# State space chunks with outputs turned in the product and the decay spread from bfloat16 parts; the first two output tiles fed piece by piece

## The reference, cut to what matters

```python
def ssd_chunked(x, dt, a, bm, cm, d_skip):
    xd = (x * dt[..., None]).reshape(bsz, nc, l, g, e, p)
    da = (dt * a).reshape(bsz, nc, l, g, e).transpose(0, 3, 4, 1, 2)
    cs = jnp.cumsum(da, axis=-1)
    seg = cs[..., :, None] - cs[..., None, :]
    decay = jnp.exp(jnp.where(tril, seg, -jnp.inf))
    cb = jnp.einsum("bclgn,bcsgn->bcgls", cm, bm)
    y_diag = jnp.einsum("bcgls,bgecls,bcsgep->bclgep", cb, decay, xd)
    decay_states = jnp.exp(cs[..., -1:] - cs)
    states = jnp.einsum("bclgn,bgecl,bclgep->bcgepn", bm, decay_states, xd)
    chunk_decay = jnp.exp(cs[..., -1])
    ...  # prev: states carried over the chunks, state * chunk_decay + new
    y_off = jnp.einsum("bclgn,bcgepn,bgecl->bclgep", cm, prev, jnp.exp(cs))
    return (y_diag + y_off).reshape(bsz, s, h, p) + x * d_skip[:, None]
# even_layer
    y = y * silu(z_a); y_a = rmsnorm of each group of 256 columns of y
    u = causal_dwconv(glu_v * sigmoid(glu_g), dw_w, dw_b)       # 31 taps
    y_b = silu(layernorm(u)) * silu(z_b)
    return x + jnp.concatenate([y_a, y_b], axis=-1) @ w_out
```

## Time and profile before

| | |
|---|---|
| median of 3 executions | 3494.46 us (3489.35 to 3498.19) |
| the profiled execution, its own time | 3493.44 us |
| its span, from first to last instruction | 3491.7 us |
| granted TensorE clock, mean over the span | 0.953 |
| TensorE busy / weight loads | 3156.6 us (90%) / 2493.5 us (71%) |
| VectorE, ScalarE, GpSimd busy | 1757.9, 978.6, 836.1 us |
| `block_even` | from about 1718 to 2690 us of the span |

### The profile page before, as it was taken

How to read it: one execution, slowest core, us unless ns; L and a number is a source line. 1 busy time by engine, 2 the same in 40 slices (tenths; PEclk the granted TensorE clock), 3 DMA queues, 4 the chain that set the end, 5 groups by cost and what they waited for, 6 DMA issues and landing times. The chain is left out here.

```text
span 3491.7 us, 38580 instructions
## 1 busy us (share of the span) xinstructions
PE 3156.6 (90%) x15262; PEld 2493.5 (71%) x15262; DVE 1757.9 (50%) x2675; ACT 978.6 (28%) x1839; POOL 836.1 (24%) x500
## 2 busy tenths in 40 slices
PE   5999988888899999999899999997798999999869
PEld 3777777666687787787678787875576777777647
DVE  4234566534532132233476868786343357777751
ACT  2332344314321010011233233332131244444430
POOL 1221000341332233332233333332122221111002
PEclk8998999999899999999899999999899999999889
DMA  2112000110111111112211111111222100000011
GB/s 103 37 36 88 13 1 13 37 49 29 44 48 44 47 48 42 49 47 72 66 43 49 61 46 63 43 67 55 115 91 84 37 31 31 25 31 25 7 61 72
DMA packets 45274, 170.26 MB, mean 49 GB/s; under 512 B 5040, under 2 KB 5312, under 8 KB 43968
## 3 DMA queue, kind: packets, MB, share of 16 engines
q1 hardware_dynamic: 44832, 161.85, 13.6%
q0 software_dynamic: 288, 6.29, 0.4%
HBM read 145.06 MB, written 23.07 MB: 48 GB/s over the span
## 5 line engine op out<-in xcount | busy, mean ns | idle before, releaser
L176 PE MATMUL acc<-x_hi,w_hi 128*128 128x512 f32 x2064 | 859.6, 416 | 88.5 <-DVE x_lo L267 43.3
L169 POOL CAST w_hi<-w_raw 128x1024 fp32r<-128x1024 f32 x217 | 237.0, 1092 | 2519.3 <-PE acc L178 1464.4
L177 PE MATMUL acc<-x_lo,w_hi 128*128 128x512 f32 x2064 | 831.5, 403 | 0.0
L178 PE MATMUL acc<-x_hi,w_lo 128*128 128x512 f32 x2064 | 829.8, 402 | 0.0
L171 POOL TENSOR_TENSOR w_lo<-w_raw,w_hi 128x1024 fp32r<-128x1024 f32 x217 | 544.3, 2508 | 17.4
L176 PEld LDWEIGHTS acc<-x_hi,w_hi 128*128 128x128 f32 x2064 | 396.8, 192 | 211.1 <-issue 81.0
L178 PEld LDWEIGHTS acc<-x_hi,w_lo 128*128 128x128 f32 x2064 | 397.6, 193 | 97.8
L177 PEld LDWEIGHTS acc<-x_lo,w_hi 128*128 128x128 f32 x2064 | 398.9, 193 | 87.2 <-issue 1.2
L2225 DVE SCALAR_TENSOR_TENSOR acc<-ev_upad,cols,acc 128x1024 f32<-128x1024 f32 x232 | 298.1, 1285 | 4.2
L378 DVE TENSOR_TENSOR h<-h,acc 128x1024 f32 (+1 forms) x40 | 48.9, 1221 | 317.1 <-PE acc L178 317.1
L176 PE MATMUL aux<-x_hi,w_hi 128*128 128x512 f32 x448 | 191.9, 428 | 0.0
(11 more groups left out here) (491 smaller groups left out, 5068.5 us busy)
## 6 DMA issues: line engine op xcount, KB each, us to landing
w_raw<-in_stream SPq DMA_DIRECT2D x217, 512.0 KB, 3.4
h<-in_x SPq DMA_DIRECT2D x16, 512.0 KB, 8.7
spill_h<-h SPq DMA_DIRECT2D x8, 512.0 KB, 5.3
spill<-ev_zst SPq DMA_DIRECT2D x8, 512.0 KB, 3.1
h_even<-spill_h SPq DMA_DIRECT2D x8, 512.0 KB, 7.8
ev_zr<-spill SPq DMA_DIRECT2D x8, 512.0 KB, 3.5
spill_h<-h_even SPq DMA_DIRECT2D x8, 512.0 KB, 5.3
h<-spill_h SPq DMA_DIRECT2D x8, 512.0 KB, 6.5
```

What stands on the lines that cost most here:

```text
L169: pool.tensor_copy(k.w_hi[slot][:], k.w_raw[slot][:]).then_inc(k.w_split, 1)
L176: pe.matmul(out, w_hi, x_hi, start=start, stop=False)
L177: pe.matmul(out, w_hi, x_lo, start=False, stop=False)
L178: return pe.matmul(out, w_lo, x_hi, start=False, stop=stop)
```

## The change

- The cumulated log decays cs are split into three bfloat16 parts on VectorE (`spl`), turned once by eight bfloat16 matmuls and copied by ScalarE to csT, with a group's three parts of four heads in 12 rows of a block of 32 partitions. `decays` becomes four bfloat16 matmuls on 32 rows, one for each head, with a selection matrix `sel` as weights. GpSimd's `d_steps` and the mask matmul go; the mask is put on the scores by VectorE (cbm).
- `products` has x as weights (64 columns) and the mixed decays as moving data, so that the output comes out turned, on the partitions 0 to 63 for even heads and 64 to 127 for odd ones. The state part becomes one matmul for each head on the same output, with cp as moving data: C times the exponential of cs (ScalarE's new ecb, VectorE's new `spread`). L1897, tmp, ysb, ecs and `back` go; `add_y` stands right behind `combine`.
- The reload is issued as twelve transfers of one tile each, and TensorE takes the output tiles 0 and 1 together, block by block (`first_pair`), with the last group's total behind block 1.

The diff, cut; allocations and names of semaphores are left out:

```diff
@@ -1787,13 +1790,6 @@
...
-    def d_steps(g, c):
-        if g * TT + c:
-            pool.wait_ge(s["cbr"], g * TT + c)
-        else:
-            pool.wait_ge(s["tables"], 4)
-        pool.tensor_tensor(d4[:], k.upto.unsqueeze(1).broadcast_to([P, 4, P]), heads(da, g, c, P), ALU.mult).then_inc(s["d4_ready"], 1)
...
     def x_ends(g, c):
         if c == 0:
...
-        d_steps(g, 0)
...
-        d_steps(g, 1)
...
         for c in range(TT):
...
-            if c + 2 < TT:
-                d_steps(g, c + 2)
...
-    for i, x in enumerate((x_hi, x_lo)):
-        pool.dma_start(x[:, 0:6, :], k.spill_ya[i][:, 0:6, :]).then_inc(s["ya_back"], 16)
+    for q in range(6):
+        pool.dma_start(x_hi[:, q, :], k.spill_ya[0][:, q, :]).then_inc(back[q], 16)
+        pool.dma_start(x_lo[:, q, :], k.spill_ya[1][:, q, :]).then_inc(back[q], 16)
...
@@ -1850,6 +1843,8 @@
...
     def turn_x(g, i):
+        if i < 2:
+            pe.wait_ge(s["cs_copied"], 1)
...
@@ -1870,46 +1865,39 @@
...
     def decays(g, c):
...
-        pe.wait_ge(s["d4_ready"], g * TT + c + 1)
+        pe.wait_ge(s["ebc"], 7 * g + max(c - 1, 0))
         if c == 0:
...
-            pe.wait_ge(s["consts"], 2)
+            pe.wait_ge(s["consts"], 3)
...
-            pe.wait_ge(s["mixed"], g * TT + c)
-            if c >= 2:
-                pe.wait_ge(s["yadded"], g * TT + c - 1)
-        pe.matmul(S[0], k.ones, d4[:].rearrange("p h c -> p (h c)"), start=True, stop=False)
-        pe.matmul(four(S[0]), identr[:], maskr[:].unsqueeze(1).broadcast_to([P, 4, P]), start=False, stop=True)
-        pe.matmul(S[3][:, 256:384], cv[:, 2, cols], cv[:, 3, cols], start=True, stop=True).then_inc(s["cbr"], 1)
+            pe.wait_ge(s["cbm"], g * TT + c)
+        r = slice(32 * g, 32 * g + 32)
+        for h in range(4):
+            pe.matmul(S[0][:, h * P:(h + 1) * P], sel[r, h, :], csT[r, cols], start=True, stop=True)
+        pe.matmul(S[3][:, 0:P], cv[:, 2, cols], cv[:, 3, cols], start=True, stop=True).then_inc(s["cbr"], 1)
...
     def products(g, c):
...
+        pe.wait_ge(s["yadded"], g * TT + c)
...
         if c == 0:
...
-            pe.wait_ge(s["ysb_ready"], g * TT + c)
+            pe.wait_ge(s["cp_ready"], 7 * g + c)
...
-            pe.matmul(S[2][:, 0:256], cv[:, 3, c * P:(c + 1) * P], state[:].rearrange("p h c -> p (h c)"), start=True, stop=True)
-        for h in range(4):
-            mm = pe.matmul(S[1][:, h * 64:(h + 1) * 64], dec[:, c % 2, h, :], xtok[:, c, h * 64:(h + 1) * 64], start=True, stop=True)
+        outs = [S[1][64 * (h % 2):64 * (h % 2) + 64, h // 2 * P:(h // 2 + 1) * P] for h in range(4)]
+        for two in (range(0, 2), range(2, 4)):
+            for h in two:
+                mm = pe.matmul(outs[h], xtok[:, c, h * 64:(h + 1) * 64], dec[:, c % 2, h, :], start=True, stop=c == 0)
+            for h in two if c else ():
+                mm = pe.matmul(outs[h], state[:, h, :], cp[:, h, :], start=False, stop=True)
...
-    def back(g, c):
-        pe.wait_ge(s["ysb_ready"], g * TT + c + 1)
-        if c < TT - 1:
-            pe.wait_ge(s["mixed"], g * TT + c + 2)
-        else:
-            pe.wait_ge(s["yadded"], g * TT + c)
-        for j in range(2):
-            mm = pe.transpose(S[3][:, j * P:(j + 1) * P], ysb[:, 2 * j:2 * j + 2, :].rearrange("p h c -> p (h c)"), k.ident)
-        mm.then_inc(s["yT"], 1)
...
     def group_total(g):
...
@@ -1930,7 +1918,11 @@
...
-            pe.wait_ge(s["tables"], 4)
+            pe.wait_ge(s["tables"], 3)
+            pe.wait_ge(s["cs_split"], 6)
+            for t in range(TT):
+                mm = pe.matmul(S[t // 4][:, t % 4 * P:(t % 4 + 1) * P], spl[:, t].rearrange("p g r -> p (g r)"), k.ident_h, start=True, stop=True)
+            mm.then_inc(s["cs_turned"], 1)
...
@@ -1950,9 +1942,7 @@
...
             products(g, c)
-            feed(n // 3)
-            back(g, c)
-            feed(n - 2 * (n // 3))
+            feed(n - n // 3)
...
     def out_tile(i, xh, xl, ready):
@@ -1970,14 +1960,28 @@
...
-    def a_ready(q):
-        if q == 0:
-            pe.wait_ge(s["ya_back"], 32)
-            pe.wait_ge(s[EV[2 * EVEN_N - 1][0]], EV[2 * EVEN_N - 1][1])
-        if q == 6:
-            group_total(SSD_GROUPS - 1)
-            pe.wait_ge(s["y_hi"], SSD_GROUPS)
-            pe.wait_ge(s["y_lo"], SSD_GROUPS)
+    def first_pair():
...
+        pe.wait_ge(s[EV[2 * EVEN_N - 1][0]], EV[2 * EVEN_N - 1][1])
+        pe.wait_ge(s["yadded"], TT * SSD_GROUPS)
+        for q in range(KD):
+            if q < 6:
+                pe.wait_ge(back[q], 32)
+            else:
+                pe.wait_ge(s["y_hi"], SSD_GROUPS)
+                pe.wait_ge(s["y_lo"], SSD_GROUPS)
+            for i in range(2):
+                n = oa + i
+                if q == 0:
+                    pe.wait_ge(k.w_split, n * 2 + 2)
+                for c in range(2):
+                    cols = slice(c * HALF, (c + 1) * HALF)
+                    mm = product3(pe, slots[i][:, cols], k.w_hi[n % 2][:, q * P:(q + 1) * P], k.w_lo[n % 2][:, q * P:(q + 1) * P],
+                                  x_hi[:, q, cols], x_lo[:, q, cols], q == 0, q == KD - 1)
+                if q == KD - 1:
+                    mm.then_inc(k.lin_done, 1)
+            if q == 1:
+                group_total(SSD_GROUPS - 1)
...
     def nothing(q):
...
@@ -2072,6 +2079,9 @@
...
+        if c:
+            act.wait_ge(s["cp_ready"], 7 * g + c - 1)
+            act.activation(ecb[:].rearrange("p h c -> p (h c)"), S[0], ACT.Exp).then_inc(s["ebc"], 1)
...
     def square(g):
...
@@ -2115,11 +2124,12 @@
...
-            act.activation(ecs, cs, ACT.Exp).then_inc(s["tables"], 1)
...
+            act.wait_ge(s["cs_turned"], 1)
+            act.activation(csT[:], aux[:, 0:SEQ], ACT.Copy).then_inc(s["cs_copied"], 1)
...
@@ -2193,7 +2203,13 @@
...
-    dve.tensor_scalar(maskr[:], k.upto, -1.0, 2.0 ** 127, ALU.add, ALU.mult).then_inc(s["consts"], 1)
+    dve.memset(spl[:], 0.0).then_inc(s["cs_split"], 1)
+    dve.tensor_reduce(picks[:], k.ident.rearrange("p (g r) -> p g r", r=32)[:, :, 0:12].rearrange("p g (i h) -> p h g i", h=4),
+                      AX, ALU.add).then_inc(s["consts"], 1)
+    dve.wait_ge(s["consts"], 1)
+    dve.tensor_reduce(onehot[:], picks[:], AX, ALU.add).then_inc(s["consts"], 1)
+    dve.wait_ge(s["consts"], 2)
+    dve.tensor_copy(sel[:], onehot[:].unsqueeze(2).broadcast_to([P, 4, P])).then_inc(s["consts"], 1)
...
     def handler(i):
@@ -2251,33 +2267,35 @@
...
     def mix(g, c):
+        dve.wait_ge(s["cbr"], g * TT + c + 1)
+        if g * TT + c:
+            dve.wait_ge(s["mixed"], g * TT + c)
+        dve.tensor_tensor(cbm, S[3][:, 0:P], k.upto, ALU.mult).then_inc(s["cbm"], 1)
+        dve.wait_ge(s["cbm"], g * TT + c + 1)
...
-        dve.tensor_tensor(dec[:, c % 2], dec[:, c % 2], S[3][:, 256:384].unsqueeze(1).broadcast_to([P, 4, P]),
-                          ALU.mult).then_inc(s["mixed"], 1)
+        dve.tensor_tensor(dec[:, c % 2], dec[:, c % 2], cbm.unsqueeze(1).broadcast_to([P, 4, P]), ALU.mult).then_inc(s["mixed"], 1)
...
+    def spread(g, c):
+        dve.wait_ge(s["ebc"], 7 * g + c)
+        dve.tensor_tensor(cp[:], ecb[:], cv[:, 3, c * P:(c + 1) * P].unsqueeze(1).broadcast_to([P, 4, P]), ALU.mult).then_inc(s["cp_ready"], 1)
...
     def combine(g, c):
...
-        if c:
-            dve.tensor_tensor(tmp[:], four(S[2][:, 0:256]), heads(ecs, g, c, 64), ALU.mult).then_inc(s["chain"], 1)
-            if c < TT - 1:
-                dve.tensor_tensor(state[:], state[:], heads(cdec, g, c, 64), ALU.mult).then_inc(s["chain"], 1)
-            dve.wait_ge(s["chain"], 13 * g + 2 * c - 1)
-            dve.tensor_tensor(ysb[:], tmp[:], four(S[1][:, 0:256]), ALU.add).then_inc(s["ysb_ready"], 1)
-            if c < TT - 1:
-                dve.wait_ge(s["chain"], 13 * g + 2 * c)
-                dve.tensor_tensor(state[:], state[:], four(S[2][:, 256:512]), ALU.add).then_inc(s["state_ready"], 1)
-                dve.wait_ge(s["state_ready"], g * (TT - 1) + c + 1)
-        else:
+        if c == 0:
...
-            dve.tensor_copy(ysb[:], four(S[1][:, 0:256])).then_inc(s["ysb_ready"], 1)
+        elif c < TT - 1:
+            dve.tensor_tensor(state[:], state[:], heads(cdec, g, c, 64), ALU.mult).then_inc(s["chain"], 1)
+            dve.wait_ge(s["chain"], 6 * g + c)
+            dve.tensor_tensor(state[:], state[:], four(S[2][:, 256:512]), ALU.add).then_inc(s["state_ready"], 1)
+        if c < TT - 1:
+            spread(g, c + 1)
...
     def add_y(g, c):
-        dve.wait_ge(s["yT"], g * TT + c + 1)
         if c == 0:
...
-        dve.tensor_tensor(yy, yy, S[3][:, 0:256].rearrange("p (j c) -> p j c", j=2), ALU.add).then_inc(s["yadded"], 1)
+        dve.tensor_tensor(yy, yy, S[1][:, 0:256].rearrange("p (j c) -> p j c", j=2), ALU.add).then_inc(s["yadded"], 1)
...
     def multiply(g):
...
@@ -2339,11 +2357,20 @@
...
+            parts = [spl[:, :, :, 4 * i:4 * i + 4] for i in range(3)]
```

(12 more changed lines are left out.)

29 lines of the change are left out of this document (17 added, 12 removed).

## The result

The changed kernel takes 3434.3 us (median of 4 runs, 3430.5 to 3441.9) beside 3491.9 us of the kernel before (4 runs): a ratio of 0.983, with a 95% interval of 0.981 to 0.985, or 57.6 us less. The forecast was 3439 us. The profiled execution took 3430.5 us around a span of 3428.7, 63.0 us shorter than that of before. Where these 63 us lie is told by marks that both traces have: the first decays, the first decays of each later group, the first tap of the last tile of `zst`, the last input product, the first of the sums over eight tiles (L1998 before, L2005 after).

The account below looks back on a forecast made before the run. TensorE's queue was taken to set the pace; 20.9 + 7.8 + 11.5 - 2.5 + 18 = 55.7 us off the profiled 3493.4 gave 3437.7, plus 1.0 to the median: 3439 us, range 3424 to 3467.

Parts of the forecast that it names:

- the rival by which the gain comes back there: At the three group changes, TensorE's waits for ScalarE take back the gain of groups 0 to 2: 3460 us; chance 0.07.
- Decays: TensorE's decay visit in each chunk: 0.80 us (0.65 to 1.14) instead of 1.32, 0.52 saved, tiling change taken at 0.35.
- Products: TensorE's product visit in each chunk: 1.63 us instead of 1.76, 0.13 saved, column halves side by side at 0.053 an entry.
- rival of halves in turn: In the product visits, column halves run one after another at 0.107 an entry: 3461 us; chance 0.17.
- A chunk: TensorE's work in one chunk: decays 0.52, products 0.13 and turn back 0.22 saved, 0.87 us together.
- Groups 0 to 2: The 24 chunks of these groups: 0.87 us saved in each, 20.9 us together, TensorE still leading.
- Slower by the tiling: In 64 visits, changing the tiling costs far more than 0.35 us; at 1.5 a visit 3513 us; chance 0.04.
- Chunks 0 to 3 of group 3: The first chunks of group 3: TensorE's waits of 1.7 + 1.5 + 1.1 go, and 4 x 0.87: 7.8 us saved.
- Last tile's stretch: Group 3, last tile's first taps to last input product: 34.4 us instead of 45.9, 11.5 saved, VectorE late without idle.
- First group: Once, ahead of the first decays: extra VectorE steps, small matmuls and a wait for ScalarE's copy cost 2.5 us (1 to 4).
- Seam: Behind the last input product: 36.8 us instead of 55.8, first wait some 5; 19.0 saved, taken as 18.
- rival of transfers that land together: At the seam, the twelve small transfers land together near 2452.7, 44.8 us instead of 37.8: 3446 us; chance 0.08.

Follow-up runs that it names:

- seam alone: The kernel before with only the new seam (twelve one-tile transfers, first two output tiles together, last group's total behind q = 1): 3470.3 us, 0.9952 of before.

## Why the prediction was right, and where it was off

- **Bound.** Right: TensorE's queue sets the pace of groups 0 to 2, and its starts, not its lengths, give the cost of a visit. From the third chunk of each group on the period is 10.80 (10.8 forecast), and the group changes kept their price, so the rival by which the gain comes back there falls.
- **Decays.** 0.66 us behind the first start and 0.09 ahead of it (2013.42 - 2013.10 - 0.23), 0.75 in all; forecast 0.80 with both. The mis-sized term is the price of changing the tiling, taken at 0.35: it is 0.23. The entries were right (0.24 for four, taken as 4 x 0.06); the score matmul and the return to the dense products take 0.28, taken as 0.21.
- **Products.** 1.56 us and again 0.09 ahead, 1.65; forecast 1.63. The reason given, halves side by side at 0.055 an entry, was right. That the sum is so near is partly luck: the tiling cost some 0.23 instead of 0.35 (0.09 ahead, and 1.02 from the first entry to L1899 where 16 x 0.055 are 0.88), and L1899 with the return to dense products 0.54 instead of 0.43. A group's last chunk has 16 entries (four rows of x4 from 2380.61 on), not the eight that the prediction says; only its first has eight. The rival of halves in turn (0.107) falls with the run that puts them in turn, and with it what it drew on: the Trainium skill, "TensorE: Matmul & The Clock Gate", Part 3, The mechanism, has weight loads overlap running matmuls only across row groups. Here both halves are on the same rows, and the entries start at twice the rate; for these entries the measurement decides.
- **A chunk.** 3.30 - 0.75 - 1.65 = 0.90 us saved, and the period went from 11.69 to 10.80; forecast 0.87.
- **Groups 0 to 2.** 24.0 instead of 20.9. 24 x 0.90 are 21.6. Of the other 2.4, two periods in each group had been 0.29 and 0.07 longer before (11.98 and 11.76 instead of 11.69), 1.1 in all; with GpSimd's subtraction in four parts the kernel before has 11.69 there too, so that was VectorE held by GpSimd. And from the last decays of a group to the first of the next, where visits lie too, 2.4, 1.5 and 1.0 us are saved (99.2, 98.2 and 97.7 before, 96.8, 96.7 and 96.7 after). Up to the long wait 1.26 are saved each time, which are the visits; the rest, 1.1, 0.2 and -0.2, is the clock behind the wait. The same products took 6.03, 5.08 and 4.56 us before, at a granted clock of 0.50, 0.61 and 0.70, and 4.93, 4.85 and 4.78 after, at 0.63 to 0.66. So about 1 us of the gain here is luck of the clock.
- **Slower by the tiling.** That rival needed 1.0 us above 0.35 a visit; measured is 0.23 in all.
- **Chunks 0 to 3 of group 3.** 9.6, forecast 7.8: the waits for VectorE went, as said. In the kernel before this stretch is 0.9 shorter with the subtraction in four parts, in the changed one it isn't, so 0.9 of the 1.8 is again VectorE held by GpSimd; the other 0.9 stays open.
- **Last tile's stretch.** 38.0 us, forecast 34.4: the worst term. VectorE is late and hasn't any idle time, as said, but its work was priced from operations that nothing disturbs. Two of them were held by GpSimd's subtraction, a mix with 1.50 instead of 0.69 and a state step with 1.53 instead of 0.42: 1.9 us. With GpSimd's subtraction in four parts the stretch is 35.2, so 2.8 of the 3.6 us are this cause with what follows from it: TensorE's two waits are 1.2 us shorter together, and the granted clock of the stretch is 0.95 instead of 0.91. What is left, 0.8, goes with the low clock behind the waits that stay (behind the wait at 2370.49 the entries start twice as far apart), which I only argue.
- **First group.** Forecast -2.5 us, without a sum of its terms; TensorE waits 2.5 us for ScalarE's copy. The trace to the first decays is 1.6 us shorter all the same, because executions differ there; the two kernels' executions that have the same granted clock at the start (1.00) begin at 1814.9 and at 1817.3 and 1818.4, so that 2.5 fits. With the copy moved ahead of the silu the wait is 0.9 shorter.
- **Seam.** 35.9 us, forecast 36.8 (saved 19.9, worked out 19.0, taken 18). First wait 5.85 (some 5), the second for GpSimd's split, no wait for the last group: all three as said. The twelve transfers took 0.52 us each to issue, not 0.62, so the split was there 10.4 us behind the input products (11.3 forecast). The 25.5 from there to the sums are the 21.0 + 4.5 of the forecast, but the 4.5 for low clock were met by luck: seam alone has 22.8 for the same products. The rival of transfers that land together falls by the first wait, and by the run that makes them land together.
- **The rest.** The profiled spans differ by 63.0 us, 61.2 between the marks of the block and 1.8 outside, while the medians differ by 57.6. The forecast took its 55.7 off the profiled execution and added the 1.0 to the median of three, which was 2.6 above the later median of four. Between the marks 61.2 are saved where 20.9 + 7.8 + 11.5 + 18 = 58.2 were forecast: +3.1, +1.8, -3.6 and +1.9. That the median came out 5 us from the forecast owes something to these errors cancelling; the mechanisms hold term by term, but for the last tile's stretch.

## What to carry to other kernels

Small float32 products with 64 output rows pay on alternating column halves: an entry costs half, and changing the tiling costs about a quarter of a microsecond a visit, so put all that is small into one visit. Before pricing an engine by its quiet operations, look for those that are two or more times as long as their like, and at what GpSimd was doing then: a long GpSimd instruction beside a VectorE path can be worth cutting, but try more than one size, as two pieces gave nothing here and four 20 us. Read a term of a few microseconds between marks of two traces, not from medians, and look at the granted clock behind each long wait before giving the rest of a difference a cause.
